# Weight slots that begin 192 bytes ahead of the moving operands, modulo 512 bytes

## The chip, the cores and the metric

One core of one Trainium2 chip runs the kernel. The time is that of the device in microseconds (us), of the one core that takes part; smaller is better. A core has TensorE (PE in the profile; its weight loads are shown apart as PEld), VectorE (DVE), ScalarE (ACT), GpSimd (POOL) and SyncE (SP, which here issues most transfers). All work from SBUF, a memory of 128 partitions in which every tensor has a first byte that is the same in each partition. TensorE writes its products into eight banks of another memory, 512 float32 numbers wide.

## What is computed

The reference is a stack of transformer blocks on 512 rows (S) of 1024 numbers (D), all in float32. Cut to what matters:

```
first block (x, 1024 wide):
  n = rms_norm(x);  z = n @ w_in                    # 1024 -> 1968
  gated linear attention (4 heads) and latent attention (8 heads, chunk mask)
  x = x + [o_g, o_m] @ w_out
  x = x + square(relu(rms_norm(x) @ w_mlp_up)) @ w_mlp_down      # 1024 -> 4096 -> 1024
  x = x + (p @ w_ple_proj) * sigmoid(rms_norm(x) @ w_ple_gate + b)
second block, two layers:
  x = x + pool_mixer(rmsnorm(x))                    # layer 0: windows 2, 4, 8, 16
  x = x + chunk_attention(rmsnorm(x))               # layer 1: 16 heads, relative bias
  each layer then:
  x = x + (silu(conv3(h @ w_gate)) * (h @ w_val)) @ w_out,  h = rmsnorm(x)   # 1024 -> 2816 -> 1024
```

Most of the arithmetic is in products of 512 rows with weight matrices of some 1024 by 256 at a time.

## The kernel before

**High and low parts.** TensorE works here on float32 numbers in a form that keeps fewer digits (`fp32r`, R in the code). To keep the precision, each operand is split into a high part, the number rounded to that form, and a low part, what is left of it. A product of weights and activations is made of three: high by high, high by low, low by high, all added up in one bank. In the code `triple` (lines 722 to 724) does this with the weights as the stationary operand, which TensorE loads 128 by 128, and the activations as the moving one, which passes by it with 512 columns. `triple_t` (lines 728 to 730) has the roles the other way round: the activations are loaded, the weights move with 256, 384 or 512 columns. A row of the profile such as `bank<-AH,WH` names first the moving operand and then the stationary one.

**Weights.** They come in units of up to 128 x 2048 numbers (8 KB a partition), in the order of the list `PLAN`. SyncE loads a unit into one of two slots RAW; ScalarE copies it into one of three slots WH (line 1486), VectorE subtracts and writes the low part into WL (line 1907). A unit is thus loaded from HBM once, split once, and used by 48 products or so. The three slots WH lie behind one another, and so do those of WL; WHR and WLR are other names for the same bytes, as a ring of twelve quarters of a slot.

**Activations.** AH and AL hold the high and low parts of the normalised rows, transposed, with 8 blocks of 512 columns. HH and HL hold the hidden numbers of the feed-forward parts, OH/OL and OM/LM outputs of attention, pH/pL the input p, cqb the inputs of the latent projections. All these begin at byte 256 modulo 512: AH and AL by the sizes of what lies ahead of them, the others since the function `in_step` rounds their place up to such a byte. The weight slots, too, begin at byte 256 modulo 512 in the kernel before. A block of 128 stationary columns is 512 bytes, so nearly every operand within a tensor keeps the first byte of its tensor modulo 512.

**Combined units.** In the first feed-forward part, eleven of the sixteen units of w_mlp_up are multiplied in seven products of half size, with sums of blocks of the weights and of the activations (`form_product`, lines 1180 to 1182, `fast_products`). They have 256 moving columns. Four of the seven have AH and AL as the moving operand, three have TH and TL, which hold sums of blocks of the activations. TH and TL begin 192 bytes later than `in_step` would put them, at byte 448 modulo 512, which the two lines with 192 in the function `memory` do. They lie over the room of pj, xg and others, which are used at other times.

**Order.** Each engine has its program written out by hand, and semaphores between them. While TensorE uses one unit, the next are split and loaded. The change touches the function `memory` alone, which gives every tensor its place: `Arena.tile` puts tensors one behind the other, `Arena.over` lays one over others.

Of the kernel before, what the change touches and what calls it, by code (L numbers as in the profile page):

```python
# [235 lines left out]
def in_step(at):  # L236

    return (at + 255) // 512 * 512 + 256


def memory(nc, ctx):
    k = Kit()
    a = Arena(nc, (nc.sbuf_base + 63) // 64 * 64, nc.sbuf_usable_end)
# [8 lines left out]
    k.AL = a.tile("AL", [P, 8, S], R)  # L252
    raw_at = a.at
    k.RAW = [a.tile(f"RAW{i}", [P, UE]) for i in range(NR)]
    wh_at = a.at
    k.WH = [a.tile(f"WH{i}", [P, UE], R) for i in range(NW)]
    wl_at = a.at
    k.WL = [a.tile(f"WL{i}", [P, UE], R) for i in range(NW)]
# [69 lines left out]
    inner = a.at = in_step(a.at)  # L328
# [1 line left out]
    k.pH = a.tile("pH", [P, 2, S], R)  # L330
    k.pL = a.tile("pL", [P, 2, S], R)
    k.pj = a.tile("pj", [P, 8, S])
    a.at += 192
    shapes_at = inner + 192
    k.TH = a.over("TH", [P, 4, 3, 256], shapes_at, R)
    k.TL = a.over("TL", [P, 4, 3, 256], shapes_at + 4 * 12 * 256, R)
    k.xg = a.over("xg", [P, 2, S], shapes_at + 4 * 24 * 256)
# [2491 lines left out]
def build(nc, W, XT, PT, PV, ROW, GW2, POS, REL, CST, MSK, BND, OUT):  # L2829
    with ExitStack() as ctx:  # L2830
        k = memory(nc, ctx)
        k.W, k.XT, k.PT, k.PV, k.ROW, k.GW2, k.POS, k.REL, k.CST, k.MSK, k.BND, k.OUT = W, XT, PT, PV, ROW, GW2, POS, REL, CST, MSK, BND, OUT
        for program in (tensor_program, vector_program, scalar_program, pool_program, sync_program):
            program(k, Dry())
        for c in (k.MM, k.WHI, k.WLO, k.ACT, k.DVE, k.POOL):
            c.n, c.known = 0, True
        block = ctx.enter_context(nc.Block())

        @block.sync
        def _(e):  # L2840
            sync_program(k, e)

        @block.tensor
        def _(e):
            tensor_program(k, e)

        @block.vector
        def _(e):
            vector_program(k, e)

        @block.scalar
        def _(e):
            scalar_program(k, e)

        @block.gpsimd
        def _(e):
            pool_program(k, e)
# [97 lines left out]
```

## Time and profile before

| | |
|---|---|
| median of 3 runs | 1640.39 us (1639.22 to 1640.83) |
| profiled execution | 1641.01 us |
| its span, first to last instruction | 1639.0 us |
| TensorE busy | 1627.2 us (99%), 8480 products |
| VectorE busy | 1028.9 us (63%) |
| ScalarE busy | 660.0 us (40%) |
| granted clock of TensorE, mean share | 0.997 |
| moved by DMA | 156.00 MB, 95 GB/s |

The span is what the profile of one execution shows between the first and the last instruction; the time of an execution has some 2 us around it. Products on TensorE overlap: the next one starts before the last has left the array, so the busy time is the union of them, and the mean duration of one (389 ns for most) is longer than the time from one start to the next. What a product costs in a row of products is the difference of the starts, which the timeline shows to a hundredth of a us; over many products that gives it to a fraction of a nanosecond.

### The profile page before, as it was taken

Reading aid. Unit: us, or ns where it says so; the run is one execution under the profiler, and the core shown is the slowest. Engines: PE = TensorE matmul, PEld = TensorE weight load, DVE = VectorE, ACT = ScalarE, POOL = GpSimd, SP = SyncE. Lnnn points to the kernel's source line nnn. Section 1 sums busy time; section 2 is a strip of 40 time slices with the busy share of each in tenths; the row PEclk is TensorE's granted clock in tenths of the full one; section 3 lists DMA queues with packets and bytes.
Section 4 is the critical chain, followed back from the end, with each engine's and each line's share of the span. In section 5 each row is a group of like instructions: output and inputs, shape, how many; then the busy total and the mean of one; then the engine's idle time right before and its main releaser. Section 6 shows DMA issues by size and latency. Waiting matters only on the chain.

```text
span 1639.0 us, 20167 instructions
## 1 busy us (share of the span) xinstructions
PE 1627.2 (99%) x8480; PEld 1349.0 (82%) x8480; DVE 1028.9 (63%) x1545; ACT 660.0 (40%) x919; POOL 84.4 (5%) x80
## 2 busy tenths in 40 slices
PE   9999999999999999999999999999999999999999
PEld 7877878898989788888888888877777888888887
DVE  6797673796867757577466457545655577366353
ACT  5576435354444446433222223355555333122121
POOL 1300000000000000000000000311201100000000
PEclk9999999999999999999999999999999999999999
DMA  5310228356464521223322322323221222222311
GB/s 187 114 38 27 104 78 135 69 109 136 85 137 84 138 102 52 77 103 106 126 84 96 103 84 101 123 78 101 77 76 52 78 103 104 102 103 90 112 62 71
DMA packets 28058, 156.00 MB, mean 95 GB/s; under 512 B 3712, under 2 KB 5392, under 8 KB 12096
## 3 DMA queue, kind: packets, MB, share of 16 engines
q1 hardware_dynamic: 26352, 149.75, 25.5%
q0 software_dynamic: 1328, 4.86, 5.5%
q8 instruction: 67, 1.10, 0.3%
q14 instruction: 23, 0.19, 0.0%
q10 hardware_dynamic: 288, 0.10, 0.0%
HBM read 149.98 MB, written 4.72 MB: 94 GB/s over the span
## 4 chain that ended last, share of the span: by engine, by line
PE 76%; DVE 2%; ACT 1%; issue 1%; POOL 0%; DVEq 0%; ACTq 0%
PE bank L722 19%; PE bank L723 19%; PE bank L724 19%; PE bank L728 3%; PE bank L730 2%; PE bank L729 2%; PE bank L1180 2%; PE bank L1182 2%; PE bank L1181 2%; PE bank L1417 1%; PE bank L1427 1%; PE bank L1443 1%; PE bank L1303 0%; ACT WH L1486 0%; PE bank L1405 0%
## 5 line engine op out<-in xcount | busy, mean ns | idle before, releaser
L1907 DVE TENSOR_TENSOR WL<-RAW,WH 128x2048 fp32r<-128x2048 f32 (+2 forms) x122 | 273.0, 2243 | 180.2 <-ACT WH L1486 180.2
L722 PE MATMUL bank<-AH,WH 128*128 128x512 f32 (+1 forms) x974 | 382.7, 393 | 0.5 <-DVE AL L1946 0.3
L724 PE MATMUL bank<-AH,WL 128*128 128x512 f32 (+1 forms) x974 | 379.2, 389 | 0.0
L723 PE MATMUL bank<-AL,WH 128*128 128x512 f32 (+1 forms) x974 | 379.1, 389 | 0.0
L1486 ACT ACTIVATE WH<-RAW 128x2048 fp32r<-128x2048 f32 (+2 forms) x122 | 227.0, 1867 | 172.4 <-PE bank L724 143.7
L722 PE MATMUL bank<-HH,WH 128*128 128x512 f32 x608 | 237.4, 391 | 3.7 <-DVE HL L2436 2.8
L723 PE MATMUL bank<-HL,WH 128*128 128x512 f32 x608 | 237.3, 390 | 0.0
L724 PE MATMUL bank<-HH,WL 128*128 128x512 f32 x608 | 237.1, 390 | 0.0
L722 PEld LDWEIGHTS bank<-AH,WH 128*128 128x128 f32 (+1 forms) x974 | 182.5, 187 | 41.7 <-issue 2.4
L724 PEld LDWEIGHTS bank<-AH,WL 128*128 128x128 f32 (+1 forms) x974 | 182.5, 187 | 38.8
L723 PEld LDWEIGHTS bank<-AL,WH 128*128 128x128 f32 (+1 forms) x974 | 182.6, 187 | 38.2 <-issue 1.0
L722 PEld LDWEIGHTS bank<-HH,WH 128*128 128x128 f32 x608 | 114.5, 188 | 28.0 <-DVE HL L2436 3.2
L724 PEld LDWEIGHTS bank<-HH,WL 128*128 128x128 f32 x608 | 114.6, 188 | 23.9
L723 PEld LDWEIGHTS bank<-HL,WH 128*128 128x128 f32 x608 | 114.5, 188 | 23.7
L1937 DVE TENSOR_TENSOR X<-X,bank 128x512 f32<-128x512 f32 x79 | 54.0, 685 | 117.0 <-PE bank L724 116.9
L1826 ACT ACTIVATE t2s<-t2s,par 128x512 f32<-128x512 f32 x44 | 31.9, 724 | 186.6 <-DVE t2s L2570 186.6
L728 PE MATMUL bank<-WH,AH 128*128 128x512 f32 x224 | 89.9, 402 | 0.0
L730 PE MATMUL bank<-WH,AL 128*128 128x512 f32 x224 | 87.5, 391 | 0.0
L729 PE MATMUL bank<-WL,AH 128*128 128x512 f32 x224 | 87.3, 390 | 0.0
L1831 ACT ACTIVATE HH<-cvs 128x512 fp32r<-128x512 f32 x44 | 27.8, 633 | 126.0 <-DVE cvs L2576 126.0
L1493 ACT ACTIVATE sq<-X 128x512 f32<-128x512 f32 x49 | 30.9, 630 | 61.0 <-DVE X L1937 57.0
L1180 PE MATMUL bank<-AH,WHR 128*128 128x256 f32 x176 | 50.3, 286 | 2.1 <-DVE X L1937 2.1
(346 smaller groups left out, 2356.7 us busy)
## 6 DMA issues: line engine op xcount, KB each, us to landing
RAW<-in_W SPq DMA_DIRECT2D x124, 1024.0 KB, 4.8
RAW<-in_W SPq DMA_DIRECT2D x9, 768.0 KB, 4.1
X<-in_XT SPq DMA_DIRECT2D x16, 256.0 KB, 5.5
ev_scratch<-ev POOLq DMA_DIRECT2D x16, 160.0 KB, 7.6
Gb<-ev_scratch SPq DMA_DIRECT2D x16, 128.0 KB, 3.2
Gb<-ev_scratch SPq DMA_DIRECT2D x16, 112.0 KB, 2.7
out<-X SPq DMA_DIRECT2D x7, 256.0 KB, 2.0
RAW<-in_W SPq DMA_DIRECT2D x2, 512.0 KB, 5.3
```

The lines of the kernel that those rows point to most:

```text
L722: e.matmul(o, a, h, start=first, stop=False)
L723: e.matmul(o, a, l, start=False, stop=False)
L724: return e.matmul(o, c, h, start=False, stop=last)
L728: e.matmul(o, h, a, start=first, stop=False)
L729: e.matmul(o, h, c, start=False, stop=False)
L730: return e.matmul(o, l, a, start=False, stop=last)
L1180: e.matmul(o, a, h, start=c == 0 and x in "ageb", stop=False, skip_group_check=True)
L1181: e.matmul(o, a, lo, start=False, stop=False, skip_group_check=True)
L1182: t = e.matmul(o, l, h, start=False, stop=c == 3, skip_group_check=True)
L1486: e.activation(k.WH[SLOT_OF[u]][:, 0:n], k.RAW[RAW_OF[u]][:, 0:n], AF.Copy).then_inc(*WHI.mark(u))
L1907: e.tensor_tensor(k.WL[j][:, 0:n], k.RAW[RAW_OF[u]][:, 0:n], k.WH[j][:, 0:n].bitcast(F), SUB).then_inc(*WLO.mark(u))
L1937: e.tensor_tensor(X[:, m, :], X[:, m, :], src, ADD).then_inc(*DVE.mark("x", n, m))
```

## The change

The weight slots are moved up by 320 bytes (320 = 512 - 192), to byte 64 modulo 512; everything that lies behind them moves up with them, and what goes through `in_step` (from gq and HH on) comes to byte 256 modulo 512 again, 512 bytes further up. The moving operands thus begin at byte 256 and the weights at byte 64, 192 bytes ahead. The two lines that set TH and TL 192 bytes further are taken out; TH and TL begin at byte 256 now, and their distance to the weights stays what it was. The buffers rb, sq, stage, dg and t2s, which lie between the weights and the first use of `in_step`, go from byte 256 to byte 64 modulo 512. Every engine's instructions are the same and stand in the same order; only addresses differ, and the line numbers behind the removed line are one lower.

```diff
--- before.py
+++ after.py
@@ -252,7 +252,7 @@
     k.AL = a.tile("AL", [P, 8, S], R)
     raw_at = a.at
     k.RAW = [a.tile(f"RAW{i}", [P, UE]) for i in range(NR)]
-    wh_at = a.at
+    wh_at = a.at = a.at + 320
     k.WH = [a.tile(f"WH{i}", [P, UE], R) for i in range(NW)]
     wl_at = a.at
     k.WL = [a.tile(f"WL{i}", [P, UE], R) for i in range(NW)]
@@ -330,8 +330,7 @@
     k.pH = a.tile("pH", [P, 2, S], R)
     k.pL = a.tile("pL", [P, 2, S], R)
     k.pj = a.tile("pj", [P, 8, S])
-    a.at += 192
-    shapes_at = inner + 192
+    shapes_at = inner
     k.TH = a.over("TH", [P, 4, 3, 256], shapes_at, R)
     k.TL = a.over("TL", [P, 4, 3, 256], shapes_at + 4 * 12 * 256, R)
     k.xg = a.over("xg", [P, 2, S], shapes_at + 4 * 24 * 256)
```

## Rows read from the trace of the kernel before

**Rows 1.** The page: span, busy time of the engines, chain that ended last

```profile
span 1639.0 us, 20167 instructions
...
PE 1627.2 (99%) x8480; PEld 1349.0 (82%) x8480; DVE 1028.9 (63%) x1545; ACT 660.0 (40%) x919; POOL 84.4 (5%) x80
...
PE 76%; DVE 2%; ACT 1%; issue 1%; POOL 0%; DVEq 0%; ACTq 0%
```

**Rows 2.** Stretches: length, busy us of each engine, granted clock, DMA share, GB/s

```profile
321.00:341.00 20.00, 19.96 (x100) 16.84 (x98) 17.37 (x21) 5.89 (x7) 0.00 (x0) 1.00 0.30 105
...
540.00:551.00 11.00, 8.18 (x37) 6.43 (x35) 6.51 (x6) 7.29 (x8) 0.54 (x1) 1.00 0.87 200
800.00:900.00 100.00, 100.00 (x443) 82.84 (x442) 55.48 (x64) 26.06 (x23) 0.00 (x0) 1.00 0.27 95
1155.00:1180.00 25.00, 24.38 (x149) 18.13 (x147) 14.13 (x33) 14.38 (x27) 5.21 (x2) 1.00 0.16 55
```

**Rows 3.** Groups by form on PE: count, busy, mean, idle before

```profile
L722 PE MATMUL bank<-AH,WH 128*128 128x512 f32 x967 | 379.9, 393 | 0.2 <-DVE X L1937 0.2
...
L722 PE MATMUL bank<-HH,WH 128*128 128x512 f32 x608 | 237.4, 391 | 3.7 <-DVE HL L2436 2.8 <-DVE t1s L2414 0.9
...
L728 PE MATMUL bank<-WH,AH 128*128 128x512 f32 x224 | 89.9, 402 | 0.0
...
L1180 PE MATMUL bank<-AH,WHR 128*128 128x256 f32 x176 | 50.3, 286 | 2.1 <-DVE X L1937 2.1
...
L1180 PE MATMUL bank<-TH,WHR 128*128 128x256 f32 x132 | 36.8, 279 | 0.0
...
L722 PE MATMUL bank<-OH,WH 128*128 128x512 f32 x64 | 26.2, 409 | 0.0
...
L722 PE MATMUL bank<-OM,WH 128*128 128x512 f32 x32 | 14.4, 450 | 0.0
...
L728 PE MATMUL bank<-WH,HH 128*128 128x256 f32 x32 | 9.1, 285 | 0.0
...
L722 PE MATMUL bank<-pH,WH 128*128 128x512 f32 x16 | 6.8, 422 | 0.0
...
L728 PE MATMUL bank<-WH,cqb 128*128 128x384 f32 x16 | 5.5, 341 | 0.0
...
L728 PE MATMUL bank<-WH,cqb 128*128 128x512 f32 x8 | 3.1, 389 | 0.0
```

**Rows 4.** Timeline of PE, start us and us: first and last of 37 products

```profile
853.71 0.39 PE L722 MATMUL bank<-AH,WH 128*128 128x512 f32 x1
...
861.87 0.39 PE L722 MATMUL bank<-AH,WH 128*128 128x512 f32 x1
```

**Rows 5.** Timeline of PE: 21 products with TH, then 21 with AH

```profile
513.41 0.28 PE L1180 MATMUL bank<-TH,WHR 128*128 128x256 f32 x1
...
515.67 0.28 PE L1182 MATMUL bank<-TH,WLR 128*128 128x256 f32 x1
...
516.61 0.28 PE L1181 MATMUL bank<-AL,WHR 128*128 128x256 f32 x1
...
519.01 0.28 PE L1180 MATMUL bank<-AH,WHR 128*128 128x256 f32 x1
```

**Rows 6.** Timeline of PE: 28 products of 384 columns with the weights moving

```profile
45.50 0.33 PE L728 MATMUL bank<-WH,cqb 128*128 128x384 f32 x1
...
50.18 0.33 PE L728 MATMUL bank<-WH,cqb 128*128 128x384 f32 x1
```

**Rows 7.** Timeline of PE: 14 products with TH in another rhythm

```profile
347.24 0.28 PE L1181 MATMUL bank<-TL,WHR 128*128 128x256 f32 x1
...
348.77 0.28 PE L1182 MATMUL bank<-TH,WLR 128*128 128x256 f32 x1
```

**Rows 8.** Timeline of PE: 9 products from the first 64-column one on

```profile
17.44 0.40 PE L722 MATMUL bank<-AH,WH 128*64 128x512 f32 x1
...
19.29 0.39 PE L724 MATMUL bank<-AH,WL 128*128 128x512 f32 x1
```


## The prediction

> **What bounds the kernel now.** I read the page first, to find out which engine sets the time. TensorE is busy 1627.2 of 1639.0 us, and the chain that ended last lies on it for 76% of the span, with 3% on the other engines [rows 1]. Then the stretches. In the middle of the feed-forward parts TensorE has no idle time at all (800 to 900 us) while VectorE is busy 55% [rows 2]; the other three stretches there are places where something else holds it up for a while. So the time is the number of products times the time from the start of one to the start of the next (the step, below). The third view gives the number. In the groups by form the stationary operand is the weights (lines 722 to 724, 1180 to 1182) or the moving one is (728 to 730); each row shown stands for three lines with the same count, since each float32 product is made of three [rows 3].
>
> The mean duration in those groups is no price: products overlap, one takes 389 ns while the next starts earlier. The step is read from the timeline. With 512 columns and both operands at the same byte modulo 512, 36 steps take 861.87 - 853.71 = 8.16 us, 226.7 ns each [rows 4]. At 2.4 GHz (granted clock 1.00 there, rows 2) 512 columns are 213.3 ns, so 13.3 ns are paid beyond the columns. With 384 columns it is 4.68 us for 27 steps, 173.3 ns, again 13.3 above the 160.0 of the columns [rows 6]. With 256 columns and AH moving 20 steps take 519.01 - 516.61 = 2.40 us, 120.0 ns, and 256 columns are 106.7: once more 13.3 [rows 5]. The surplus does not grow with the columns; it is paid once a product.
>
> Only one pair of operands lies differently in the kernel before: TH and TL, whose first byte is 192 bytes past that of the weights modulo 512, which is what the change makes of all others. Their 20 steps take 515.67 - 513.41 = 2.26 us, 113.0 ns where the hundredths leave some 0.5 ns open [rows 5]. The shape and the weight slots are the same as those of AH, and the stretches lie 1 us apart. So the surplus is halved: 6.3 to 6.8 ns in place of 13.3. I take a gain of 6.7 ns a product.
>
> **The change part by part.** Nothing is added or taken away on any engine, no wait and no transfer moves; the order of the instructions is that of before. What changes is addresses. TH and TL keep their distance to the weights, so their 132 x 3 = 396 products [rows 3] keep their price.
> - Weights stationary, 512 columns: (967 + 608 + 64 + 32 + 16) x 3 = 5061 products [rows 3]. At 6.7 ns that is -33.9 us. This is the large term and it is an inference: TH is seen with 256 columns alone. What speaks for it is that the surplus at the same byte is the same with 256, 384 and 512 columns, so what causes it seems to be over within the first 256. The upper bound is the unsettled row: after a product with 64 stationary columns, 8 steps take 19.29 - 17.44 = 1.85 us, 231.3 ns [rows 8], 4.6 more than the settled 226.7, which would be +23.3 us. The lower one is the whole surplus of 13.3 gone, -67 us; no row with both operands streaming at 2.4 GHz is near it, so I go by TH.
> - Weights stationary, 256 columns, AH moving: 176 x 3 = 528 products [rows 3], 6.7 ns each, -3.5 us. This is the case of TH itself.
> - Weights moving: (224 + 32 + 16) x 3 = 816 products [rows 3]. Here the moving operand begins 192 bytes ahead of the stationary one, the reverse of TH. At the same byte the roles cost the same [rows 5, 6]. Bounds: -5.5 us (816 x 6.7, if the direction doesn't matter) and +3.8 us (816 x 4.6, if they fall into the unsettled step). 192 in one direction is 64 in the other modulo 256, and 13.3 ns is the time in which the moving operand passes 32 columns, 128 bytes; if 128 is the period, both directions are one case. I take half the gain, -2.7 us.
> - Where others hold the end. From 321 to 341 us VectorE is busy 17.37 of 20 us with the first combined units, and TensorE then idles 2.1 us in front of line 1180 [rows 2, 3]; from 540 to 551 us TensorE is busy 8.18 of 11 us, 3.7 us of idle stand in front of line 722 with HH [rows 2, 3]; around 1155 to 1180 us it is busy 24.38 of 25. A product that ends sooner there only waits longer. These 56 us at 2.4% are 1.3 us, and I put +1.6 us for the whole kernel. Elsewhere VectorE at 55% and DMA at 27% have room for a TensorE that is 2.4% faster; DMA is at 87% only in the stretch from 540 to 551 us, which this term holds.
> - The buffers behind the weights (rb, sq, dg, t2s) move by 320 bytes too. They feed float32 products without the high and low parts, sums and transposes, and vector work. I cost this at nothing; nothing in the rows prices it.
>
> Sum: -33.9 - 3.5 - 2.7 + 1.6 = -38.5 us. The profiled execution took 1641.0 us, so 1602.5; the median of the runs, 1640.4, lies 0.6 below it, so I forecast 1602.
>
> The Trainium skill has a rule that speaks against all of this. Its page "TensorE: Matmul & The Clock Gate", section "Step-by-step: what each phase is for", says that TensorE reads the moving operand and the weight load through two independent ports and that loading the next weights doesn't steal bandwidth from the running product; "SBUF — State Buffer", section "Who interferes with whom", says that TensorE never waits on anyone. By these the first byte could not matter, and the time would stay. The trace disagrees for 256 columns: 113.0 against 120.0 ns with the same instructions. With 512 columns no row decides it.
>
> **The rivals.**
> 1. *The step with 512 columns stays.* The load of the next weights lasts a shorter time than 512 columns, and the step could be set by what comes after it. Then only the 528 products gain: 1640.4 - 3.5 = 1637. For it: no row shows 512 columns at another distance. Against it: the equal surplus of 13.3 at three lengths. The case that an address does nothing is the same one without the 3.5, 1640.
> 2. *Products settle into another rhythm.* TH itself is seen in a second one: in the first combined unit 13 steps take 348.77 - 347.24 = 1.53 us, 117.7 ns [rows 7], a gain of 2.3 instead of 6.7. With it, (5061 + 528) x 2.3 = 12.9 us, and 1627. Against it: it is seen in that unit only.
> 3. *Slower: with 512 columns the settled step is lost.* The place is every product of 512 columns in lines 722 to 730, most of all the feed-forward parts where TensorE never idles. At the same byte the step falls into 226.7 after some eight products; on the way there it is 231.3 [rows 8], and at the other distance it may never settle. 256 columns differ: from 515.67 to 516.61 us, on the way from TH to AH, 8 steps take 117.5 ns each [rows 5], below the settled 120, so what is good for TH need not be good for 512. Price: (5061 + 672) x 4.6 = 26.4 us, less 3.5, so +23 and 1663. It decides from a step over 227.4 ns with 512 columns: 0.6 ns x 5733 outweighs the 3.5 us.
>
> **How the numbers follow.** Chances: forecast 0.55, rival 1 0.11, rival 2 0.09, rival 3 0.25. I give rival 3 that much because the large term rests on a row of another length. The forecast's own range is 1594 (moving weights gain in full, no wait lengthened, the surplus down a little more) to 1612 (moving weights lose, some units in rhythm 2). Rivals 1 and 2 lie at 1627 to 1640; to leave out no more than 0.2 the range must take in the lower half of rival 3, so it ends at 1657. A change under 0.2%, 3.3 us, can't be told from none: rival 1 lies on that edge and counts as 0.04 faster, 0.07 the same. Faster 0.55 + 0.09 + 0.04 = 0.68, the same 0.07, slower 0.25.
>
> **What the profile after would show.** The step with AH or HH moving and 512 columns, read as in rows 4, is 220.0 ns if I am right, 226.7 by rival 1, 231 by rival 3, 224.4 by rival 2. The product's own duration falls with it, from 389 to some 382 ns. AH with 256 columns goes from 120.0 to 113.3, TH stays at 113.0. The 384-column step with moving weights tells the reverse direction: 166.7 or 173.3. The number of products in 100 us of pure feed-forward work, 443 in rows 2, rises to 456. The forecast is wrong if that number stays or falls, or if the steps shrink and the idle time in front of lines 722 and 1180 grows by more than a few us.

## The result and the profile after

The changed kernel takes 1667.3 us (median of 4 runs, 1666.7 to 1669.7), the kernel before in the same runs 1639.8. The ratio is 1.0170, with a 95% interval of 1.0158 to 1.0182: 27.5 us slower, where a gain of 38 us was forecast. The time lies outside the range, which ended at 1657. What came nearest is rival 3 of the prediction, whose price was 1663; how far its mechanism held is said below.

The page of the kernel after, next to [rows 1]. TensorE sets the end as before, with more busy time for the same 8480 products; VectorE and ScalarE are as they were:

```profile
span 1664.6 us, 20167 instructions
...
PE 1654.7 (99%) x8480; PEld 1347.7 (81%) x8480; DVE 1029.0 (62%) x1545; ACT 660.3 (40%) x919; POOL 84.6 (5%) x80
...
PE 75%; DVE 3%; ACT 2%; issue 1%; POOL 0%; DVEq 0%; ACTq 0%
```

The stretches of the kernel after (columns as in [rows 2]). In the middle of the feed-forward part the row counts 430 products in 100 us where it counted 443. The other two stretches are fuller than at the same times before mainly because everything lies later by then: the wait that fell between 548.1 and 551.0 us now begins at 550.9 and is nearly as long, 2.6 us for 2.8.

```profile
341.00:347.00 6.00, 5.14 (x36) 4.62 (x36) 5.76 (x9) 1.98 (x3) 0.00 (x0) 1.00 0.16 67
540.00:551.00 11.00, 10.86 (x51) 8.63 (x50) 6.11 (x9) 7.31 (x8) 1.59 (x3) 1.00 0.80 163
800.00:900.00 100.00, 100.00 (x430) 80.74 (x429) 53.15 (x58) 24.74 (x21) 0.00 (x0) 1.00 0.24 86
```

The groups by form (line numbers are one lower than before). The mean durations of the products of 512 columns with the weights stationary are 7 and 5 ns longer than in [rows 3], those with AH and 256 columns 7 ns shorter, those with moving weights 1 ns longer:

```profile
L721 PE MATMUL bank<-AH,WH 128*128 128x512 f32 x967 | 386.3, 400 | 0.2 <-DVE X L1936 0.2
...
L721 PE MATMUL bank<-HH,WH 128*128 128x512 f32 x608 | 241.0, 396 | 3.5 <-DVE HL L2435 2.6 <-DVE t1s L2413 0.9
...
L727 PE MATMUL bank<-WH,AH 128*128 128x512 f32 x224 | 90.3, 403 | 0.0
...
L1179 PE MATMUL bank<-AH,WHR 128*128 128x256 f32 x176 | 49.0, 279 | 0.9 <-DVE X L1936 0.9
...
L1179 PE MATMUL bank<-TH,WHR 128*128 128x256 f32 x132 | 36.8, 279 | 0.3 <-DVE WLR L2444 0.3
```

The steps, read from the timeline of the kernel after, for the same stretch as [rows 4]. There are 35 steps between the first and the last row shown, 8.17 us: 233.4 ns in place of 226.7. The first three rows show durations of 0.40 and 0.39 us by turns. The starts lie 236 and 231 ns apart by turns, where before all steps were 226 or 227:

```profile
859.66 0.40 PE L721 MATMUL bank<-AH,WH 128*128 128x512 f32 x1
859.90 0.39 PE L722 MATMUL bank<-AL,WH 128*128 128x512 f32 x1
860.13 0.40 PE L723 MATMUL bank<-AH,WL 128*128 128x512 f32 x1
...
867.83 0.39 PE L723 MATMUL bank<-AH,WL 128*128 128x512 f32 x1
```

With 256 columns and AH moving, next to [rows 5]: 10 steps in 1.13 us, 113.0 ns in place of 120.0. But from 511 us on, in the third group of combined units, 27 steps take 3.18 us, 117.8 ns, the second rhythm of [rows 7]. The products with TH keep 117.8 ns there too, where they took 113.3 before:

```profile
430.04 0.28 PE L1180 MATMUL bank<-AL,WHR 128*128 128x256 f32 x1
...
431.17 0.28 PE L1181 MATMUL bank<-AH,WLR 128*128 128x256 f32 x1
...
518.50 0.28 PE L1181 MATMUL bank<-AH,WLR 128*128 128x256 f32 x1
...
521.68 0.28 PE L1181 MATMUL bank<-AH,WLR 128*128 128x256 f32 x1
```

With the weights moving, 512 columns with AH as the stationary operand: 30 steps in 6.87 us, 229.0 ns:

```profile
1113.92 0.39 PE L727 MATMUL bank<-WH,AH 128*128 128x512 f32 x1
...
1120.79 0.39 PE L727 MATMUL bank<-WH,AH 128*128 128x512 f32 x1
```

And 384 columns, next to [rows 6]: 29 steps in 5.03 us, 173.4 ns, as before:

```profile
45.21 0.34 PE L728 MATMUL bank<-WL,cqb 128*128 128x384 f32 x1
...
50.24 0.34 PE L727 MATMUL bank<-WH,cqb 128*128 128x384 f32 x1
```

So the kinds of products answered in different ways. With the weights stationary, 512 columns lost 6.7 ns a step, and 256 columns gained 6.7 or 2.2. With the weights moving, 512 columns lost 2.3 ns, and 384 neither gained nor lost.

### The profile page after: what moved, and what is told of

The parts are those of the page before. It is cut to its first block, busy times and chain, and to the rows that moved or that the text cites. A ratio compares the mean times of both kernels' runs of the same rounds, so it can differ in the third digit from the quotient of the medians.

```text
span 1664.6 us, 20167 instructions
## 1 busy us (share of the span) xinstructions
PE 1654.7 (99%) x8480; PEld 1347.7 (81%) x8480; DVE 1029.0 (62%) x1545; ACT 660.3 (40%) x919; POOL 84.6 (5%) x80
## 4 chain that ended last, share of the span: by engine, by line
PE 75%; DVE 3%; ACT 2%; issue 1%; POOL 0%; DVEq 0%; ACTq 0%
PE bank L721 20%; PE bank L723 19%; PE bank L722 19%; PE bank L727 3%; PE bank L729 2%; PE bank L728 2%; PE bank L1179 2%; PE bank L1181 2%; PE bank L1180 2%; PE bank L1416 1%; PE bank L1426 1%; PE bank L1442 1%; DVE WLR L2444 1%; PE bank L1302 0%; ACT WH L1485 0%
## 5 line engine op out<-in xcount | busy, mean ns | idle before, releaser
L721 PE MATMUL bank<-AH,WH 128*128 128x512 f32 (+1 forms) x974 | 389.1, 400 | 0.2 <-DVE X L1936 0.2
L723 PE MATMUL bank<-AH,WL 128*128 128x512 f32 (+1 forms) x974 | 385.7, 396 | 0.0
L722 PE MATMUL bank<-AL,WH 128*128 128x512 f32 (+1 forms) x974 | 385.6, 396 | 0.0
L721 PE MATMUL bank<-HH,WH 128*128 128x512 f32 x608 | 241.0, 396 | 3.5 <-DVE HL L2435 2.6
L722 PE MATMUL bank<-HL,WH 128*128 128x512 f32 x608 | 240.8, 396 | 0.0
L723 PE MATMUL bank<-HH,WL 128*128 128x512 f32 x608 | 240.8, 396 | 0.0
L2563 DVE TENSOR_TENSOR t1s<-bank,rb 128x512 f32<-128x512 f32 x44 | 30.3, 688 | 38.7 <-PE bank L723 38.7
```

Of the source, the lines that this page charges most:

```text
L721: e.matmul(o, a, h, start=first, stop=False)
L722: e.matmul(o, a, l, start=False, stop=False)
L723: return e.matmul(o, c, h, start=False, stop=last)
```

## The experiments

The theory after the result, D: the settled step of a stream of products hangs on the distance in bytes between the stationary and the moving operand and on the number of columns, and on nothing else of the change. All products called float32 here are of the form `fp32r`. Rivals: A, the weights' own byte decides; B, the buffers behind the slots do it, which the change moves too; C, any difference from the old layout costs; F, there are better distances yet.

**1. Products alone, at many distances.** One tensor per distance; the order of the stream, shortened:

```diff
+w = {d: over(f"d{d:03d}x", [P, 512], base + (256 - d) % 512, R) for d in range(0, 512, 32)}
+for d in range(0, 512, 32):            # the same again with M[:, 0:256] and M[:, 0:384]
+    for i in range(48):
+        e.matmul(bank[i % 8], w[d][:, i % 4 * P:i % 4 * P + P], M, start=True, stop=True)
+# fourth pass: N in place of M, 512 columns; N begins 64 bytes later than M
```

> Leaves out the whole computation: it copies x to the output and streams products alone, 48 in a row for each of 16 distances (the stationary operand begins 0, 32, ... 480 bytes ahead of the moving one modulo 512), with 512, 256 and 384 moving columns, and with 512 once more where both operands' first bytes are 64 later. Theory D (the distance in bytes between the two operands, together with the number of columns, sets the settled step): distance 0 gives 226.7 ns with 512 columns, 120.0 with 256, 173.3 with 384; distance 192 gives 233.3 with 512 and 113.3 or 117.7 with 256; the fourth pass, at the same distances, repeats the first within 1 ns. Rival A (the weights' own byte modulo 512 decides, not the distance): the fourth pass is the first shifted by two places of the list. Rival B (what slowed the kernel is not the weights' distance but something else of the change): distance 192 with 512 columns gives 226.7.

The kernel did not do quite what that text says of the fourth pass: only the moving operand begins 64 bytes later there, the stationary ones stay where they were. The real distance in that pass is thus 64 more than the tensor's name tells. Theory D then expects the list shifted by two places, and rival A, by which the weights' own byte decides, no shift. This is the reverse of what the text expects of the two, and it is said here with the result known; it follows from the addresses in the kernel (`M` begins at byte 256 modulo 512, `N` at 64 later, the stationary tensors are the same).

The timeline merges equal products, so that the start of one row to the start of the next, over 48, is the step (moving operand, stationary one with its distance in bytes; L53 is 512 columns with M, L56 256, L62 512 with N):

```profile
29.24 11.05 PE L53 MATMUL bank<-Mx,d000x 128*128 128x512 f32 x48
40.13 11.35 PE L53 MATMUL bank<-Mx,d032x 128*128 128x512 f32 x48
51.32 11.16 PE L53 MATMUL bank<-Mx,d064x 128*128 128x512 f32 x48
62.31 11.36 PE L53 MATMUL bank<-Mx,d096x 128*128 128x512 f32 x48
...
95.95 11.36 PE L53 MATMUL bank<-Mx,d192x 128*128 128x512 f32 x48
107.15 11.36 PE L53 MATMUL bank<-Mx,d224x 128*128 128x512 f32 x48
118.35 11.05 PE L53 MATMUL bank<-Mx,d256x 128*128 128x512 f32 x48
129.25 11.35 PE L53 MATMUL bank<-Mx,d288x 128*128 128x512 f32 x48
...
241.57 5.62 PE L56 MATMUL bank<-Mx,d192x 128*128 128x256 f32 x48
247.02 5.84 PE L56 MATMUL bank<-Mx,d224x 128*128 128x256 f32 x48
...
432.44 11.16 PE L62 MATMUL bank<-Nx,d000x 128*128 128x512 f32 x48
443.44 11.36 PE L62 MATMUL bank<-Nx,d032x 128*128 128x512 f32 x48
...
499.48 11.05 PE L62 MATMUL bank<-Nx,d192x 128*128 128x512 f32 x48
510.37 11.35 PE L62 MATMUL bank<-Nx,d224x 128*128 128x512 f32 x48
```

Distance 0: 10.89 us over 48, 226.9 ns. Distance 192: 11.20, 233.3. Distance 256: 10.90, as 0. Distance 64, which is what the moving weights have in the changed kernel (192 the other way): 10.99, 229.0. Distance 192 with 256 columns: 5.45, 113.5. In the fourth pass the short one is d192x, real distance 256, and d000x takes 11.00 as d064x did in the first. All 16 settings of the fourth pass agree within 0.1 ns with those of the first two places further on. So the list did shift by two: rival A falls, distance decides. From the single starts of the second half of each setting:

```
distance            0      32      64      96     128     160     192     224     256 ... 480
512 columns, ns   226.7   233.3   228.9   233.3   233.3   234.3   233.3   233.3   as 0 ... 224
384 columns       173.3   176.7   173.3   176.7   175.8   176.7   174.7   173.3   as 0 ... 224
256 columns       120.0   116.7   117.8   120.0   118.6   117.3   113.3   118.3   as 0 ... 224
```

The pattern repeats after 256 bytes in all three. The stream alone gives each settled step of the kernel after: 233.4, 229.0, 173.4, 113.0 (moving weights at distance 64, all others at 192). What it does not give is the 117.8 of the third group. With 512 columns distance 0 is the best of the list, and with 256 it is among the worst.

**2. The change without its side effect.**

```diff
-    wh_at = a.at
+    wh_at = a.at = a.at + 320
...
+    a.at += 192
     k.rb = a.tile("rb", [P, S])
...
-    a.at += 192
-    shapes_at = inner + 192
+    shapes_at = inner
```

> The change without its side effect: the weight slots begin 192 bytes ahead, but rb, sq, stage, dg and t2s are put back to byte 256 modulo 512. Theory D: as slow as the change, 1667 us (1665 to 1669), step 233.3 ns with 512 columns. Rival B (the buffers behind the slots do it): near the kernel before, 1637 to 1643.

1665.1 us, ratio 1.0154 (1.0138 to 1.0170). 35 steps take 8.17 us, 233.4 ns:

```profile
859.62 0.39 PE L724 MATMUL bank<-AH,WL 128*128 128x512 f32 x1
...
867.79 0.40 PE L723 MATMUL bank<-AL,WH 128*128 128x512 f32 x1
```

**3. The side effect without the change.**

```diff
+    a.at += 320
     k.rb = a.tile("rb", [P, S])
...
-    a.at += 192
-    shapes_at = inner + 192
+    shapes_at = inner
```

> The side effect without the change: the weight slots stay at the same byte as the moving operands, rb, sq, stage, dg and t2s go 192 bytes ahead, and TH and TL are at the same byte as the weights as well. Theory D: the time before plus 396 products x 6.7 ns = 2.6 us, so 1642 to 1643. Rival B: 1665 or more.

1641.5 us, ratio 1.0009 (1.0000 to 1.0019), 36 steps in 8.16 us, 226.7 ns. Rival B falls with these two. The ratio is +1.5 us, with 0 to 3.1 in the interval, where 2.6 were expected for TH; run 5 asks for it by itself.

```profile
859.63 0.39 PE L723 MATMUL bank<-AL,WH 128*128 128x512 f32 x1
...
867.79 0.39 PE L723 MATMUL bank<-AL,WH 128*128 128x512 f32 x1
```

**4. Only the high slots moved.**

```diff
+    wh_at = a.at = a.at + 320
     k.WH = [a.tile(f"WH{i}", [P, UE], R) for i in range(NW)]
-    wl_at = a.at
+    wl_at = a.at = a.at + 192
```

(TH and TL at `inner`, as in the change.)

> Only the high slots WH begin 192 bytes ahead; the low slots WL stay at the moving operands' byte. Each triple loads high, high, low, so two of three loads have the new distance. Theory D with a price for each load alone: two thirds of 33.7 us on the 5061 products of 512 columns, 1640 + 22 = 1662, within 4. Rival C (a settled rhythm that needs the same distance in every load): the step falls out of both rhythms and is 231 ns or more, as after the 64-column products: 1640 + 5061 x 4.6 = 1663 or more, with steps that differ within a triple and from the two settled values.

1671.3 us, ratio 1.0188 (1.0169 to 1.0207), at the median 4 us above the change with all slots moved; the two intervals touch. The price per load, 1662, is outside; rival C's "1663 or more" holds. But its step came out only in part. The 35 steps below take 8.16 us, 233.1 ns, which is the step of the whole change; what differs within a triple is the single step, 233.9, 231.2 and 234.9 ns behind high by high, low by high and high by low in this stretch:

```profile
859.75 0.40 PE L721 MATMUL bank<-AH,WH 128*128 128x512 f32 x1
...
867.91 0.40 PE L723 MATMUL bank<-AH,WL 128*128 128x512 f32 x1
```

The products that cost more than with the whole change are the others. Those of 256 columns lose much of what it gave them:

```profile
L1180 PE MATMUL bank<-AL,WHR 128*128 128x256 f32 x176 | 50.1, 285 | 0.0
L1179 PE MATMUL bank<-AH,WHR 128*128 128x256 f32 x176 | 49.6, 282 | 0.8 <-DVE X L1936 0.8
```

Their step is 122.5 ns in most of the first group of combined units and 117.8 in the other two. From one start to the next, added up over the trace, the 256-column products with AH take 1.9 us more than with the whole change, those with TH 1.6 and those with the weights moving 2.4. (The profiled execution, 1675.2 us, is also the slowest of the four, and TensorE's granted clock was low in it for longer.) So two distances by turns within a triple are no mean of the two: two moved loads of three cost the 512-column products as much as three.

**5. TH and TL at the weights' byte**, with nothing else changed: the two lines with 192 give way to `shapes_at = inner`.

> The kernel before with TH and TL at the same byte as the weights, everything else as it was. Theory D: 396 products of 256 columns at 120.0 in place of 113.3 ns, +2.6 us, 1643 (1642 to 1644). Rival (the distance of TH is without effect on the whole, since those stages wait for VectorE): 1640.5.

1641.3 us, ratio 1.0008 (1.0000 to 1.0017), +1.3 us with 0 to 2.8 in the interval. The granted clock of the executions tells more. In the profiled ones it falls to 1.2 GHz in one to three places behind the start, for 3.4 or 6.8 us each, and the time goes with its mean: the kernel before takes 1640.7 us at a mean of 0.997, 1639.2 at 0.998 and 1637.4 at 0.999 (7, 9 and 5 executions beside this run). At the same 0.998, nine executions of this kernel take 1641.4, 2.2 us more than the nine of before. The trace agrees: the 256-column products with AH and TH take 115.7 us from start to start where they took 113.2. So the one placement that the kernel before had by itself was worth some 2 us, near the 2.6 expected, and runs 3 and 7, which place TH alike, say the same (1.9 and 2.1 at equal clock).

**6. Slots 64 bytes ahead.** `wh_at = a.at = a.at + 448`, TH and TL at `inner`.

> The weight slots begin 64 bytes ahead of the moving operands instead of 192, TH and TL at the same distance. By the settled steps that the streams of products alone showed: 5061 products of 512 columns with the weights stationary at 228.9 instead of 226.7, +11.1 us; with the weights moving the distance is 192, 672 x 6.7 = +4.6; 528 products of 256 columns with AH at 117.8 instead of 120.0, -1.2; 396 with TH at 117.8 instead of 113.3, +1.8. Theory D: +16.3 us, 1657 (1654 to 1660), between the kernel before and the change. Rival C (any distance but 0 loses the rhythm): as slow as the change or slower, 1665 or more.

1651.1 us, ratio 1.0072 (1.0059 to 1.0085), +11.7 us. It lies between the two kernels as D has it, and rival C in its strong form falls. But 1657 was too much, and its range, from 1654, was missed. The settled step is the expected one, 35 steps in 8.01 us, 228.9 ns. The shortfall is spread over the terms; from start to start, added up over the trace, the kinds changed by +10.0 us where +11.1 was expected (512 columns, weights stationary), +3.4 for +4.6 (weights moving) and -1.4 for +0.6 (256 columns, AH and TH together), the last mostly because the clock fell once less among them. That products which have just started or changed operands are not settled in either kernel would explain the first two; it was not tested by itself. The mean durations by form:

```profile
859.77 0.39 PE L721 MATMUL bank<-AH,WH 128*128 128x512 f32 x1
...
867.78 0.39 PE L723 MATMUL bank<-AH,WL 128*128 128x512 f32 x1
```

```profile
L721 PE MATMUL bank<-AH,WH 128*128 128x512 f32 x967 | 381.4, 394 | 0.2 <-DVE X L1936 0.2
...
L1179 PE MATMUL bank<-TH,WHR 128*128 128x256 f32 x132 | 36.8, 279 | 0.0
```

**7. Slots 256 bytes ahead.** `wh_at = a.at = a.at + 256`, TH and TL at `inner`.

> The weight slots begin 256 bytes ahead, TH and TL too. Theory D with a period of 256 bytes: the same step as at the same byte, 226.7 ns with 512 columns, and the whole as the kernel with TH at the same byte, 1643 (1641.5 to 1644.5). Rival (the period is 512 bytes, as the byte chosen for the activations suggests): the step leaves 226.7 and the time is above 1650.

1641.1 us, ratio 1.0008 (1.0000 to 1.0017), the same as run 5, which has TH and TL placed alike. 36 steps in 8.16 us, 226.7 ns. In the kernel, too, the period is 256 bytes:

```profile
859.81 0.39 PE L722 MATMUL bank<-AL,WH 128*128 128x512 f32 x1
...
867.97 0.39 PE L722 MATMUL bank<-AL,WH 128*128 128x512 f32 x1
```

**8. Finer distances, fewer stationary columns, other lengths.** The stream of run 1 with one stationary tensor read from a start that goes back by one number at a time, then with 32 to 128 stationary columns, then with 128 to 512 moving ones. Shortened:

```diff
+e.matmul(bank[i % 8], f[:, 16 - x + i % 4 * P:...], M)        # 4 x bytes ahead, x = 0 ... 15
+e.matmul(bank[i % 8][0:n], w[d][:, i % 4 * P:i % 4 * P + n], M) # n = 32, 64, 96, 128; d = 0, 192
+e.matmul(bank[i % 8][:, 0:n], w[d][...], M[:, 0:n])            # n = 128 ... 512; d = 0, 64, 192
```

> Leaves out the whole computation: it copies x to the output and streams products alone, 48 in a row for each setting: first 512 columns with the stationary operand 0, 4, ... 60 bytes ahead; then 512 moving columns with 32, 64, 96 and 128 stationary columns at distance 0 and 192; then 128 to 512 moving columns at distance 0, 64 and 192. Theory D': the surplus over the columns comes from the load of the next weights reading beside the moving operand, so it hangs on the distance modulo 256 and on how long the load lasts. Expected: some distances within a 64-byte block give steps between 226.7 and 233.3, none under 220; fewer stationary columns shrink the surplus, at both distances, to under half at 32 columns; at distance 0 every multiple of 128 columns has 13.3 ns of surplus, and at 192 the surplus goes from 6.7 with 256 columns to 20.0 with 512 by way of 384 (14.7 seen before). Rival E (the surplus is a fixed time between products that only a phase rounds up): it does not change with the number of stationary columns.

```
stationary columns        32      64      96     128      (512 moving, ns)
distance 0              231.7   230.0   230.0   226.7
distance 192            231.1   232.6   228.3   233.3

moving columns           128     192     256     320     384     416     448     480     512
distance 0              111.7   111.7   120.0   146.7   173.3   188.3   206.7   216.7   226.7
distance 64             111.7   111.7   117.8   146.7   173.3   188.3   200.0   218.3   228.9
distance 192            111.7   111.7   113.3   146.7   176.7   186.7   202.2   216.1   233.3
```

(Means of 24 settled steps.) The 4-byte distances give 226.7 ns at 0 and 4, and 228.3 to 236.7 from 8 to 60 bytes, so 233.3 is not the top, as D' had it. The part of D' that names the cause falls: with 32 stationary columns the surplus over 213.3 ns is 18 ns at either distance, not under half, though the load itself is shorter, 109 ns in the trace for the 188 with 128 columns. How long the load lasts does not set it. Nor does a fixed pause that a phase rounds up (rival E), since the surplus does change with the stationary columns, in both directions. The equal surplus of 13.3 ns at distance 0 is not general either: it is there at 256, 320, 384 and 512 columns, but it is 20.0 at 448 and 58 at 128. In the order of the lengths there is no rule that could be carried from 256 to 512: at distance 192 the surplus is 6.6, 13.4, 16.7, 13.4, 15.5, 16.1 and 20.0 ns at 256, 320, 384, 416, 448, 480 and 512 columns.

**9. Every distance, and bfloat16.** The same stream with 64 starts 4 bytes apart, 512 and 256 columns, and eight distances with both operands in bfloat16.

> Leaves out the whole computation: it copies x to the output and streams products alone, 36 in a row for each setting: the stationary operand 0, 4, ... 252 bytes ahead of the moving one, with 512 columns and then with 256, and 0, 32, ... 224 bytes ahead with 512 columns and both operands in bfloat16. Theory D (distance modulo 256 sets the settled step; 226.7 at distance 0 is the lowest for 512 columns, 113.3 at 192 the lowest for 256): no setting is below 226 with 512 columns or below 113 with 256. Rival F (there are better distances between the 32-byte steps): some setting is at 220.0 or less with 512 columns, which would make the kernel before faster by 30 us or more. For bfloat16, half the bytes per column: if the surplus comes from how fast float32 operands are read, all distances give about 216 ns or less and no two differ by over 1 ns; if it belongs to any product at 2.4 GHz, they spread as the float32 ones do, by 5 ns or more.

```profile
23.06 535.85 PE L59 MATMUL bank<-Mx,fine 128*128 128x512 f32 x2304
558.75 272.55 PE L62 MATMUL bank<-Mx,fine 128*128 128x256 f32 x2304
831.13 62.33 PE L65 MATMUL bank<-Bx,half 128*128 128x512 bf16 x288
```

With 512 columns the mean over all 64 distances is (558.75 - 23.06) / 2304 = 232.5 ns. The lowest is 226.7, at 0, 4, 124 and 136 bytes, the highest 243.3 at 100. Rival F falls: with all products at one distance, none that is a multiple of 4 bytes makes a settled 512-column step shorter than in the kernel before. (Distances that differ within a triple were tried once, in run 4.) With 256 columns the mean is 118.2, the lowest 113.3, at 52, 76, 88, 180 and 204 bytes. Distance 192 gave 117.8 in this run, and 113.3 in runs 1 and 8; with 384 columns it gave 174.7 in run 1 and 176.7 in run 8. So the distance and the columns do not settle the step alone, as D had it. The tensors and what ran before them differ between these streams. In the kernel after, the same products with the same distance take 113.3 in one group of units and 117.8 in the next; what makes the difference was not tested. In bfloat16 the 288 products take 62.3 us, 215.8 ns a step at each of the eight distances: the low and equal steps that were expected if the surplus comes from how float32 operands are read. That does not show that it does. The Trainium skill gives in "TensorE: Matmul & The Clock Gate", section "Back-to-back issue gap", for a single product on an engine at the higher clock a gap of the columns at 2.4 GHz and 2.5 ns, 215.8 with 512 columns; the trace agrees for bfloat16, in a stream too, and for no float32 setting of 512 columns here. The some 131 ns that the same section gives for a stream of loads and products of 512 columns no run here shows.

## Why the prediction was wrong

**The step that failed** is the large term: weights stationary, 512 columns, 5061 products at 6.7 ns, -33.9 us. The rows showed the halved surplus for 256 columns, and the prediction carried it to 512 because the surplus at the same byte was 13.3 ns at 256, 384 and 512. That equality is one of distance 0, and not of every length there (run 8). At distance 192 the surplus is 6.6 at 256 and 20.0 at 512 (runs 1 and 8). The term had the wrong sign and, by the settled steps, the very size: 5061 x 6.7 = +33.9 us; no run ties the two sizes together. A gain carried over from another length was the step without a row of its own.

**What it amounted to.** Durations overlap, so the sum goes by the starts: the time from each start to the next, added up over the trace by kind. All products with the weights stationary and 512 columns took 29.8 us more than before, 18.1 of it those with AH (6.2 ns each) and 10.1 those with HH (5.5 ns each). With 256 columns it was -3.1 with AH and -1.4 with TH, with the weights moving +0.7, and all else -0.5. Together this is 25.5 of the 25.6 us by which the profiled span grew.

**Weights stationary, 256 columns, AH**: -3.5 us forecast; the step fell from 120.0 to 113.3 as said, but to 117.8 only for 156 of the 528. From start to start it came to -3.1 us, of which some 1 is what the clock gave (below). Right in the main. TH was to stay at 113.0; in the third group its 108 products went to 117.8, some 0.5 us.

**Weights moving**: -2.7 us forecast between -5.5 and +3.8. Measured 229.0, 173.4 ns and, with 256 columns, 2 ns shorter, +0.7 us together from start to start. Within the bounds, with the other sign than the 2.7; the count of 816 leaves out the 8 x 3 products of the last row of [rows 3], 0.1 us. The guess that 128 bytes is the period was wrong, it is 256 (runs 1 and 7), so the reverse direction is a distance of 64 and not 192.

**Where others hold the end**: the term was sized for a faster TensorE. With a slower one it turned round: in front of the combined units TensorE waited 0.9 us in place of 2.1 [rows 3]. Its clock stayed at 2.4 GHz there, the 1.00 of the first row of the stretches after, where the kernel before had a mean of 0.72 behind its longer wait. It also stayed there behind the wait in front of the products with HH, where in the kernel before it fell to 1.2 GHz. Two rows of the kernel before and one of the kernel after (the clock is the third number from the right):

```profile
341.00:347.00 6.00, 3.92 (x20) 3.92 (x21) 5.92 (x8) 3.94 (x6) 0.00 (x0) 0.72 0.00 0
551.00:555.00 4.00, 4.00 (x11) 3.14 (x12) 2.42 (x4) 0.63 (x1) 0.00 (x0) 0.57 1.01 414
```

```profile
551.00:557.00 6.00, 3.55 (x15) 2.92 (x16) 4.84 (x6) 0.63 (x1) 0.00 (x0) 1.00 0.99 394
```

Each of the two stretches at 1.2 GHz lasts 3.4 us in the trace, and products of 256 columns take 213 ns in the first, so one costs some 1.5 us (an estimate from these rows). The first belongs to the change: of the eight profiled versions of the kernel, the four in which TensorE waited 2.1 us there have the fall, and the four in which it waited 0.8 to 1.7 us have not. The second does not: the wait in front of HH is 2.6 to 2.8 us in all eight, and three have the fall. So the shorter wait gave back some 1.5 us, and the comparison of these two traces some 1.5 more by chance. The sums above contain both. The prediction had no term for the clock.

**The buffers behind the slots** at nothing: right, as far as the runs tell. Run 3 moves them and TH together and costs 1.5 us by the ratio, with 0 to 3.1 in the interval; run 5, with TH alone, costs 1.3. The runs leave 2 us between the change and the slots alone, 1667.3 and 1665.1, whose intervals overlap.

**The rivals.** Rival 3 came nearest: the step with 512 columns lies above 227.4, and where it priced +23 the kernel lost 27.5. Its mechanism was half right. The settled step was lost, but what came was another settled step, 233.3 ns, and not an unsettled one of 231; and its 672 products with moving weights lost 2.3 ns a settled step, not 4.6. That its price lies within 5 us is in part luck, since these two misses and the clock work against each other. Its own warning, that unsettled steps lie above the settled one at 512 columns and below it at 256, pointed the right way, and a chance of 0.25 looks too little for it: the argument on the other side was one row of another length.

**What stays open** is what makes the surplus. It is there in float32 and not in bfloat16, and it hangs on the distance modulo 256 bytes, on both column counts, and at times on something more, which may be what ran before. The load's length alone was ruled out; how the reads of the two operands meet was not seen by any run. Nor was a kernel tried in which AH alone has another distance in the 256-column products than in the 512-column ones: both read the same slots, which other units fill in turn, and it could bring 528 x 6.7 = 3.5 us at most. No version here beats the kernel before.

## What to carry to other kernels

Where a kernel is one long stream of float32 products in the form `fp32r`, look at the distance of stationary and moving operand modulo 256 bytes. It made 2.9% of the settled 512-column step here and 1.7% of the kernel's time, and it must be measured for the very shape that the stream has: the best distance for 256 columns was the wrong one for 512. Measure it with a stream of products alone, 48 at each distance, which gave the settled steps of the real kernel to 0.5 ns but for the second rhythm with 256 columns, and weigh the steps by the number of products of each shape. Do not carry a gain from one shape to another because they agree at one setting.

## What the runs showed of the hardware that was not expected

- The settled step of an `fp32r` product of 512 columns at 2.4 GHz runs from 226.7 to 243.3 ns with the first bytes alone (run 9), and repeats after 256 bytes (runs 1 and 7). In bfloat16 it is 215.8 at all eight distances tried (run 9).
- Distance and columns do not always settle it: with 256 columns and distance 192 the step was 113.3 or 117.8 ns, in streams and within one kernel.
- Many of the settled steps fall on the same few values, 3.3 ns apart: 226.7, 230.0 and 233.3 with 512 columns, 113.3, 116.7 and 120.0 with 256; others, as 117.8 and 228.9, are means of uneven patterns. In the streams of runs 1 and 8 they are reached within ten products.
- Products of 128 and of 192 columns take the same 111.7 ns at three distances (run 8). So at these lengths something other than the columns sets the step.
- Loading fewer stationary columns does not shorten a 512-column step: 226.7 with 128, 230.0 with 64, 231.7 with 32 at distance 0 (run 8).
- The same wait of 2.6 to 2.8 us on TensorE was followed by a fall of the granted clock to 1.2 GHz in three of eight profiled kernels. A fall lasted 3.4 or 6.8 us.
